# Rings of weight slots: five split slots made four units ahead, four raw slots

## The reference

```python
qkv = rms_norm(x) @ w_qkv;  x = x + attention(qkv) @ w_o
x = x + (silu(h @ w_gate) * (h @ w_up)) @ w_down
mod = silu(c) @ ada_w[l] + ada_b[l]          # shift, scale, gate
h = modulate(rmsnorm(x, g_pre[l]), shift, scale)
proj = h @ a_w_in;  y = mlstm(proj) @ a_w_out
kv = hkv @ kv_w;  y = (band_attention(h @ b_w_in, kv) * silu(z)) @ b_w_out
x = x + gate * rmsnorm(y, g_post[l])
```

## Time and profile before

| | |
|---|---|
| median of 3 runs | 2430.07 us (2429.83 to 2431.5) |
| profiled execution | 2430.13 us, its span 2428.4 us |
| mean granted TensorE clock | 0.999 of full speed |
| TensorE matmuls, weight loads | 99%, 81% of the span |
| VectorE, ScalarE, GpSimd | 71%, 48%, 2% |
| DMA | 578.14 MB, mean 238 GB/s |
| ScalarE's L1541 idle for TensorE | 908.2 us in 597 waits |

### The profile page before, as it was taken

How to read it: one execution, slowest core, us unless ns; L and a number is a source line. 1 busy time by engine, 2 the same in 40 slices (tenths; PEclk the granted TensorE clock), 3 DMA queues, 4 the chain that set the end, 5 groups by cost and what they waited for, 6 DMA issues and landing times.

```text
span 2428.4 us, 30812 instructions
## 1 busy us (share of the span) xinstructions
PE 2412.7 (99%) x11321; PEld 1965.9 (81%) x11321; DVE 1726.5 (71%) x2422; ACT 1169.8 (48%) x1583; POOL 45.2 (2%) x65
## 2 busy tenths in 40 slices
PE   9999999999999999999999999999999999999998
PEld 7777888888888888778888888888888778888887
DVE  8885777777777776678678667677676676666665
ACT  6665444444444444544444434444444564455553
POOL 1000000000000000000000000000000000000000
PEclk9999999999999999999999999999999999999999
DMA  8445788888888887467777787767777557776654
GB/s 299 140 131 165 262 296 292 302 295 296 285 295 293 290 294 240 156 224 239 240 230 234 242 263 239 243 231 241 232 236 241 158 191 254 242 238 211 233 191 138
DMA packets 161828, 578.14 MB, mean 238 GB/s; under 512 B 18288, under 2 KB 20592, under 8 KB 161680
## 3 DMA queue, kind: packets, MB, share of 16 engines
q1 hardware_dynamic: 160432, 572.64, 71.3%
q0 software_dynamic: 1104, 3.28, 0.5%
q10 hardware_dynamic: 144, 0.26, 0.0%
HBM read 574.01 MB, written 2.10 MB: 237 GB/s over the span
## 4 chain that ended last, share of the span: by engine, by line
PE 94%; DVE 3%; ACT 1%; issue 1%; DMA 1%; POOL 0%; SPq 0%; DVEq 0%; ACTq 0%
PE PS L1167 30%; PE PS L1169 29%; PE PS L1168 29%; DVE WL L2153 1%; PE PS L791 1%; ACT WH L1541 0%; PE PS L898 0%; DMA X<-in_x 0%; PE PS L871 0%; PE PS L798 0%; PE PS L886 0%; DVE X L2120 0%; PE PS L994 0%; PE PS L1068 0%; PE PS L1014 0%
## 5 line engine op out<-in xcount | busy, mean ns | idle before, releaser
L2153 DVE TENSOR_TENSOR WL<-W,WH 128x1024 fp32r<-128x1024 f32 x814 | 990.6, 1223 | 530.5 <-ACT WH L1541 527.6
L1541 ACT ACTIVATE WH<-W 128x1024 fp32r<-128x1024 f32 x814 | 857.4, 1060 | 919.5 <-PE PS L1169 908.2
L1167 PE MATMUL PS<-WH,XTH 128*128 128x512 f32 x2144 | 855.7, 399 | 2.3 <-DVE XTL L1672 1.2
L1169 PE MATMUL PS<-WH,XTL 128*128 128x512 f32 x2144 | 835.9, 390 | 0.0
L1168 PE MATMUL PS<-WL,XTH 128*128 128x512 f32 x2144 | 835.1, 390 | 0.0
L1167 PEld LDWEIGHTS PS<-WH,XTH 128*128 128x128 f32 x2144 | 402.8, 188 | 93.1 <-issue 10.9
L1169 PEld LDWEIGHTS PS<-WH,XTL 128*128 128x128 f32 x2144 | 402.4, 188 | 85.5
L1168 PEld LDWEIGHTS PS<-WL,XTH 128*128 128x128 f32 x2144 | 403.1, 188 | 83.5 <-issue 3.8
L1167 PE MATMUL PS<-WH,YTH 128*128 128x512 f32 x1120 | 441.1, 394 | 2.9 <-DVE WL L2153 1.8
L1169 PE MATMUL PS<-WH,YTL 128*128 128x512 f32 x1120 | 436.2, 390 | 0.0
L1168 PE MATMUL PS<-WL,YTH 128*128 128x512 f32 x1120 | 436.0, 389 | 0.0
(11 more groups left out here) (282 smaller groups left out, 1181.7 us busy)
## 6 DMA issues: line engine op xcount, KB each, us to landing
W<-in_vec SPq DMA_DIRECT2D x192, 512.0 KB, 4.5
W<-in_avoz SPq DMA_DIRECT2D x192, 512.0 KB, 4.5
W<-in_wg SPq DMA_DIRECT2D x88, 512.0 KB, 4.6
W<-in_wu SPq DMA_DIRECT2D x88, 512.0 KB, 4.8
W<-in_wd SPq DMA_DIRECT2D x88, 512.0 KB, 4.8
W<-in_gate SPq DMA_DIRECT2D x64, 512.0 KB, 4.5
W<-in_aqk SPq DMA_DIRECT2D x64, 512.0 KB, 4.5
W<-in_aout SPq DMA_DIRECT2D x64, 512.0 KB, 4.4
```

The lines of the kernel that those rows point to most:

```text
L1167: e.matmul(p, x, WH[:, g % NH, j], start=first, stop=False)
L1169: i = e.matmul(p, y, WH[:, g % NH, j], start=False, stop=last)
L1541: e.activation(WH[:, n % NH], W[:, i % NW], ACT.Copy).then_inc(s_hi, 1)
L2153: e.tensor_tensor(l, src, h.bitcast(F32), ALU.subtract).then_inc(s_lo, 1)
```

## The change

Three numbers: two raw slots fewer, one split slot more, and the work of splitting stands one unit further ahead in the order of ScalarE and VectorE. A raw slot has 4 KB in each partition and a split slot 4 KB in each of WH and WL, so the memory is the same. All waits follow from the numbers; no line else is touched.

```diff
-NW = 6
-NH = 4
-LOOK = 3
+NW = 4
+NH = 5
+LOOK = 4
```

## The result

The changed kernel takes 2439.65 us (median of 6 runs, 2437.97 to 2440.72), against 2429.95 us for the kernel before on the same chip. The ratio is 1.0039, 95% interval 1.0029 to 1.0048: 9.7 us slower, beyond the upper end of the predicted range. The profiled execution took 2440.32 us, its span is 2438.6 us. All times are medians of undisturbed executions; one of the kernel with four raw slots alone took 5590.06 us, over twice the rest, and is left out.

A forecast was written before the change was run, and what follows sets the result against it. TensorE, 99% busy at an even matmul pitch, was taken as the bound: 2430.13 - 0.8 - 0.2 + 0.5 + 0.4 = 2430.0 us. The range was 2427.0 to 2433.5 us.

The forecast's parts named there:

- Four raw slots: 250 to 970 us: ring turns in 6.2 to 7.2 us against 7.18 needed, cushion covers late tiles; term 0.
- rival 2: 250 to 970 us: ring of four too short, lag adds up; landing 4.72 uses up cushion, 4.9 gives 2448 us; chance 0.09.
- At 444 us: Rows of c: whole chain one unit earlier, half there 2 us before needed, TensorE's wait goes; -0.8 us.
- The start, term +0.4: Before unit 8: X load stands behind a waiting raw slot, lands at about 26.6; +0.4 us, bounds 0 and +2.
- rival 4: Start costs more: key and value work behind conversions whose slots land late, no cushion; 2434 us; chance 0.03.
- The gates, term +0.5: Vector item ahead of VectorE's first gate steps: +0.9, less 0.2 each at L957 and L994; net +0.5 us.
- what was at no cost: Waits beside the norms: VectorE's scaling no earlier, TensorE will wait at the transpose instead; 0, bounds 0 to -2.5 us.
- Worth something only where TensorE waits for a half: Five split slots, four units ahead: cushion grows from 5.7 to 8.4 us, useful only at such waits; -0.8 and -0.2 us.
- The rule on DMA time: Raw slot landing estimated 3.2 us, unit's slot 5.7 us, term 0 with ease; prediction noted it counts one transfer alone.

The follow-up runs named there:

- the run with the filled wait: Changed kernel with nine more matmuls of ones on TensorE right ahead of its wait for unit 8; 2440.52 us, ratio 1.0042.

## Why the prediction was wrong

**Which step failed.** The step "Four raw slots", with its term of 0 from 250 to 970 us. It asked whether four slots turn as fast on average as TensorE needs them, and answered with a landing that would fall to 3.7. The landing stayed at 4.7, where rival 2 put its border, and even so TensorE lost nothing between 480 and 720 us. The average was just enough and did not settle the time. The ring of four has almost no reserve: behind one standstill of VectorE (7 to 9 us for the rows of c) two tiles are there in place of four, and what follows comes at the pace of the landing. With nothing else changed four raw slots cost 7.2 us, most of it at this place, and five cost nothing that can be told. (The 258 us with three are another matter: that ring turns too slowly all along.) Rival 2 had the right resource and the wrong arithmetic: it added up lag turn by turn, where in the changed kernel the whole of it arose at one place. Yet it was nearer than the forecast in one thing: with the standstill taken away and the stream 5% denser, the cushion did drain turn by turn, from 8.4 us to 0.7.

**"At 444 us", term -0.8.** It was the same mistake from the other side: it moved the chain one unit earlier and left the ring out. The loads of c were issued 434.41 - 431.92 = 2.5 us later than before, of which 3.2 us come from the start; so the chain gained 0.7 us, not 2.7. They took 9.8 us, not 8.0. And the order with LOOK 4 put the vector item in front of L1879. I had looked for such a move at the gates, and at the rows of c only on ScalarE, not on VectorE. The place costs +7.3; 5.5 to 6.4 with LOOK 4 behind a better start, 5.1 with LOOK 3 (4.5 late at unit 156, from 0.6 early).

**The start, term +0.4.** The mechanism was right: the load of X stands behind the raw slot that waits. The size was not: X landed 1.3 us later, not 0.4, and unit 17 is 3.2 us late. The step had the first ten transfers land as before; but the raw slot in front of X was issued at 22.86, not 22.33, and X landed 4.7 us behind that, where the sum had 4.3. The 3.2 us are beyond the bound of +2, near rival 4's twice that. In the run with the filled wait TensorE waited for the key and value work, which is the reason that the bound gave. The order has a share: with the same four raw slots and LOOK 3 in the early slots unit 17 is 0.0 to 1.3 us late.

**The gates, term +0.5, and what was at no cost.** L948 waits 0.75, and L957 and L994 have left the list: right. At the norms the wait for a low half went over to L820, as the step on them said: right, 0 within 1 us.

**The fifth split slot.** "Worth something only where TensorE waits for a half" was right as a rule. But the waits for halves were to come from the raw ring, and there it gives back 3.5 us. LOOK 4, which the prediction took for the same thing as the deeper ring, costs 6.0, since it puts every item's work, also that of items whose tile has not landed, ahead of a step that TensorE waits for.

**The rule on DMA time.** The page "SBUF — State Buffer", section "The DMA setup-cost knee", of the Trainium skill gives about 2 us plus the bytes over 436 GB/s, an estimated 3.2 us for a tile. With four slots the median was 3.6 from 100 to 205 us and 4.7 from 480 to 720. The trace comes near it from 100 to 205 us, and not in the stretch on which the term rested.

**Still open.** Why the loads of c took 9.8 us with LOOK 4 and 8.5 with LOOK 3 (both with four raw slots) is open. And LOOK 4 was not run with six raw slots, since with its five split slots that needs 8 KB in each partition more than either kernel uses, so how much LOOK 4 costs where tiles are always there is not known. Nor is it known whether an order of the stream exists in which four raw slots cost nothing: each of the three kernels with four raw slots and moved vector items lost time elsewhere in the dense stretch.

## What to carry to other kernels

Size a ring of prefetched tiles not only by whether it turns fast enough on average, but also by the longest standstill of the engine that frees its slots: count how many tiles are landed when it moves again, and how long the next takes. A busy table, the mean traffic and the landing time showed nothing of this; it took the first ten conversions behind the standstill, and the cushion from unit to unit. Then keep two things apart that look like one number: a deeper ring gives cover, and a longer look-ahead in the order of an engine puts work that may wait for memory ahead of steps that need nothing but the engine. Where the tiles may be late, deepen the ring and leave the order alone.

## What the runs showed of the hardware

- After a wait of 5.57 us TensorE's granted clock was 0.54 from 450 to 455 us; after one of 1.94 us at 28.8 us it was 0.50 from 32 to 34 us, with matmuls 0.42 to 0.43 us apart. After one of 1.41 us at the same place, in the kernel with four raw slots alone, it stayed at 1.00. With nine matmuls in the wait it stayed at 1.00 too.
- The landing of a tile of 0.5 MB in the dense stretch was 4.7 us (median) with six slots, 4.8 with five, 4.7 with four and 4.5 with three: it hardly changed with the number of slots.
- Runs of kernels with four raw slots spread more: 2429.7 to 2435.4 us in 11 runs of the one with LOOK 3, against 2429.3 to 2431.5 in 21 runs of the kernel before. That without reserve a landing that is late by chance arrives at TensorE would explain it; no run shows it by itself.
